# A mixture-of-experts trunk: the index products of a later turn moved from before the down products to behind the transposes

## Chip, cores and metric

One core of a Trainium2 chip runs the whole program in one launch. The metric is the device time in microseconds, the median of several runs. Inputs, weights and arithmetic are f32, except for small one-hot and index tables in bf16.

## What is computed

The reference is a trunk of two layers on 1024 tokens of 1024 features. The first layer mixes tokens with windowed attention, the second with a Fourier transform, and both end with a mixture of 64 experts, of which each token takes 8. The change lies in the experts alone:

```
flat_e = top_e.reshape(-1)
order = jnp.argsort(flat_e)
e_s, tok_s, w_s = flat_e[order], flat_tok[order], flat_w[order]
...
def body(y, b):
    rows = lax.dynamic_slice_in_dim(tok_buf, b * MOE_BLOCK, MOE_BLOCK)
    wb = lax.dynamic_slice_in_dim(w_buf, b * MOE_BLOCK, MOE_BLOCK)
    e = block_e[b]
    xb = x_pad[rows]
    hb = jax.nn.silu(xb @ w_gate[e]) * (xb @ w_up[e])
    return y.at[rows].add((hb @ w_down[e]) * wb[:, None]), None
```

## The kernel before

**Turns.** The routed rows are packed into turns of 128 rows, 71 a layer, in the order of a table (`ORDER`) that gives the experts and of a table (`UNITS`) that gives each expert's rows in units of 32. `schedule` packs them; a turn holds the rows of one or two experts. `pieces` cuts a turn into column tiles of TensorE: one piece 128 wide if the turn has one expert, else pieces 64 or 32 wide. The width is a matter of each turn, so that neighbouring turns and the turn four ahead often have different widths. Rows beyond the tables' capacities go through a loop behind the last turn, which a table of overflow blocks steers.

**One turn b on TensorE** (the block `pe` of `experts`, loop at L1811): `gate_up(b, par, range(SPLIT))`, the first five of eight column steps of gate and up (L1750, 512 columns each, f32, into `exG`); `turn_hidden(b - 1)`, two transposes of the hidden rows of the turn before (L1772, `exH`); the last three column steps of gate and up; `index(b + 4)`, the small products that give the row numbers and weights of the turn four ahead (L1718, `exI`, 6 columns in bf16, 8 steps for each piece); and `down(b - 1)`, the down products (L1784, `exD`). For the turn T - 4 `index_over` takes the place of `index` (L1727).

**What stands around it.** `index(b + 4)` waits for the one-hot tile that DVE makes (`onehot`, L1502, in the trace `mod<-place,slots`; `onehot_over`, L1509, for the last), and for the copy of the index products before (L1517). DVE's turn is `onehot(b + 4)`, `turn_blocks(b + 2)` (L1538), `hidden(b)` (L1543 to L1547, after gate and up of turn b and ACT's exponential, L1683), `indices(b + 4)` (L1517 to L1525), `targets(b - 1)` (L1583) and `weigh(b - 1)` (L1576). In turn 9 `overflow()` stands ahead of `onehot`, 25 small instructions (L1592 to L1617). ACT's turn is `turned(b - 1)`, which copies the transposed hidden rows for down (L1688), `gates(b)` (L1683) and `move(b + 2)` (L1671). POOL gathers the rows of later turns by `indices` and adds the weighed rows into DRAM. SP loads an expert's gate and up weights once the turn that used that ring slot last is through gate and up, and its down weights once that turn's down is through. All of this is written out by hand; the same order of the calls holds on every engine whatever the data.

The loop's order on TensorE is in these lines:

```
gate_up(b, par, range(SPLIT))
turn_hidden(b - 1, 1 - par)
gate_up(b, par, range(SPLIT, KT))
...
if b + AHEAD < T:
    index(b + AHEAD, par)
...
down(b - 1)
```

Of the kernel before, what the change touches and what calls it, by code (L numbers as in the profile page):

```python
# [26 lines left out]
KT = D // P  # L27
# [71 lines left out]
def after(eng, sem, s, lag):  # L99

    if not isinstance(s, int) or s >= lag:
        eng.wait_ge(sem, s - lag + 1)
# [35 lines left out]
def pieces(turn):  # L138

    m = P if len(turn) == 1 else 2 * UNIT if turn[1][3] == 2 * UNIT else UNIT  # L140
    return [(s, r, p, m) for s, r, _, at, n in turn for p in range(at, at + n, m)]
# [61 lines left out]
def trunk(nc, A, out):  # L203
# [9 lines left out]
    with ExitStack() as whole:  # L213
# [1141 lines left out]
        def experts(layer, place, moving, ids, skey, ring, slots, small, w_in, wd_in, load_in, load_down, expert, spent,  # L1355
# [4 lines left out]
            T = len(turns)  # L1360
            GP, GB = T % 2, T // 2
            with ExitStack() as ctx:
# [31 lines left out]
                HAND, AHEAD, SPLIT, Q = 2, 4, 5, P // UNIT  # L1394
# [10 lines left out]
                def columns_ready(eng, b):  # L1405

                    if isinstance(b, int) and HAND <= b < T:
                        eng.wait_ge(moved, b - HAND + 1)
                    else:
                        n = b + 1 if isinstance(b, int) and b < HAND else b - T + 1 + HAND  # L1410
                        eng.wait_ge(xT_a, n)
                        eng.wait_ge(xT_d, n)

                def row(eng, g, c, hi):
                    return eng.value_load(table[0:1, ds(g * 4 + c, 1)], min_val=0, max_val=hi)
# [5 lines left out]
                with nc.Block(no_gpsimd_drain=True) as block:  # L1421
# [75 lines left out]
                    def _(dve):  # L1497
                        def onehot(b, par):

                            after(dve, idx_mm, b, 2)  # L1500
                            for _, r, start, at, n in turns[b]:
                                last = dve.tensor_tensor(hot[:, par, :, at:at + n], place[:, :, r:r + 1].to_broadcast([P, NT, n]),  # L1502
                                                         slots[:, start:start + n].unsqueeze(1).to_broadcast([P, NT, n]), ALU.is_equal)
                            last.then_inc(hot_done, 1)
# [206 lines left out]
                    def _(pe):  # L1711
                        def index(b, par):
                            pe.wait_ge(hot_done, b + 1)
                            if b >= 1:
                                pe.wait_ge(idx_own, 3 if b == 1 else b * 4 - 2)
                            for t in range(NT):
                                for _, r, p, m in pieces(turns[b]):
                                    last = pe.matmul(psI[p:p + m, 0:6], hot[:, par, t, p:p + m], moving[:, t, r, :],  # L1718
                                                     start=t == 0, stop=t == NT - 1)
                            last.then_inc(idx_mm, 1)  # L1720

                        def index_over(b, g):
                            r = row(pe, g, 0, E - 1)
                            pe.wait_ge(hot_done, b + 1)
                            pe.wait_ge(idx_own, b * 4 - 2)
                            for t in range(NT):
                                last = pe.matmul(psI[:, 0:6], hot[:, GP, t], moving[:, t, ds(r, 1), :].rearrange("p a c -> p (a c)"),  # L1727
                                                 start=t == 0, stop=t == NT - 1)
                            last.then_inc(idx_mm, 1)

                        def turn_rows(b, par, landed_at):
                            pe.wait_ge(gathered[par], landed_at)
                            if not isinstance(b, int) or b > T:
                                columns_ready(pe, b - 1)
                            elif b > 0:
                                columns_ready(pe, min(b - 1, HAND - 1))
                            for k in range(KT):
                                last = pe.transpose(psX[:, k], xg[:, par, k * P:(k + 1) * P], ident[:])
                            last.then_inc(X_mm, 1)

                        def gate_up(b, par, some):
                            if some[0] == 0:
                                for s, _, _, _, _ in turns[b]:
                                    if first[s] == b:
                                        pe.wait_ge(w_in[s % RING], 32 * (s // RING + 1))
                                columns_ready(pe, b)
                                after(pe, h_done, b, 2)
                            for k in some:
                                for s, _, p, m in pieces(turns[b]):
                                    last = pe.matmul(psG[par][p:p + m], xT[:, par, k, p:p + m], ring[s % RING][:, 0:2, k * FF:(k + 1) * FF],  # L1750
                                                     start=k == 0, stop=k == KT - 1)
                            if some[-1] == KT - 1:
                                last.then_inc(g_mm, 1)
# [14 lines left out]
                        def turn_hidden(b, par):  # L1768
                            pe.wait_ge(h_done, b + 1)
                            after(pe, hT_done, b, 1)  # L1770
                            for k in range(FK):
                                last = pe.transpose(psH[:, k * P:(k + 1) * P], hid[:, par, k * P:(k + 1) * P], ident[:])  # L1772
                            last.then_inc(H_mm, 1)

                        def down(b):
                            for s, _, _, _, _ in turns[b]:
                                if first[s] == b:
                                    pe.wait_ge(wd_in[s % RING], 16 * (s // RING + 1))
                            pe.wait_ge(hT_done, b + 1)
                            after(pe, y_done, b, 1)  # L1780
                            for c in range(2):
                                for k in range(FK):
                                    for s, _, p, m in pieces(turns[b]):
                                        last = pe.matmul(psD[p:p + m, c], hT[:, k * P + p:k * P + p + m],  # L1784
                                                         ring[s % RING][:, 2, k * D + c * 512:k * D + (c + 1) * 512],
                                                         start=k == 0, stop=k == FK - 1)
                            last.then_inc(d_mm, 1)
# [23 lines left out]
                        for b in range(1, T):  # L1811
                            par = b % 2
                            gate_up(b, par, range(SPLIT))
                            turn_hidden(b - 1, 1 - par)
                            gate_up(b, par, range(SPLIT, KT))
                            if b + 1 == T:
                                turn_rows(T, 1 - par, (T // 2 + 1) * 16)
                            if b + AHEAD < T:
                                index(b + AHEAD, par)
                            elif b + AHEAD == T:  # L1820
                                pe.wait_ge(table_in, 16)
                                index_over(T, 0)
                            down(b - 1)
                        turn_hidden(T - 1, 1 - GP)
                        down(T - 1)
# [545 lines left out]
```

## Time and profile before

| | us |
|---|---|
| median of 3 runs | 2861.16 |
| lowest and highest | 2856.9, 2862.29 |
| profiled execution, its own time | 2862.66 |
| its span | 2860.8 |
| TensorE busy in the span | 2691.1 (94%) |
| DVE busy | 1847.5 (65%) |
| ACT busy | 1350.4 (47%) |
| mean granted clock of TensorE | 0.976 |

The experts take the span from about 770 to 1586 us in the first layer and from about 1980 to 2801 in the second. A matmul's end is modelled in the profile, so that the duration of a row of the timeline is longer than the time to the next product: distances between starts are what counts. A row of the timeline that merges several products gives the first start, the time to the last one's end and their count (an f32 product of 512 columns stands there as two).

### The profile page before, as it was taken

What the parts mean: (1) busy time and instruction counts of PE and PEld (TensorE: products, weight loads), DVE (VectorE), ACT (ScalarE), POOL (GpSimd) and SP (SyncE); (2) the same over time, 40 slices, a digit from 0 to 9 for tenths busy, and PEclk for the clock granted to TensorE, in tenths of its full rate; (3) what the DMA queues carried; (4) which work ended last, traced back from release to release, by engine and by line L of the source; (5) the groups of instructions that cost most, each with busy time, mean ns of one, the idle gap of its engine ahead of it and who ended that gap; (6) DMA issues with size and microseconds to landing.
All of it is one profiled execution on the core that took longest, in us unless ns stands there. A gap on an engine that the chain in (4) does not pass through costs nothing. (4 is left out here: it accounts for less than half of the span.)

```text
span 2860.8 us, 40299 instructions
## 1 busy us (share of the span) xinstructions
PE 2691.1 (94%) x14086; PEld 1224.5 (43%) x14087; DVE 1847.5 (65%) x3359; ACT 1350.4 (47%) x3130; POOL 506.4 (18%) x404
## 2 busy tenths in 40 slices
PE   7998999899899999999999698997999999999994
PEld 2444666445333433434434274443333334333332
DVE  4995555566667666666765545666676766666655
ACT  1113555201166666666665340012656666666653
POOL 0000000111022222222222211100222222222212
PEclk9999999999999999999999899998999999999997
DMA  9777300201499999999999622016999999999996
GB/s 356 269 266 214 125 16 8 80 30 45 170 358 349 334 317 349 357 355 344 378 335 309 225 89 87 30 44 238 330 322 329 306 373 358 349 379 294 330 342 206
DMA packets 147092, 714.98 MB, mean 250 GB/s; under 512 B 16702, under 2 KB 22078, under 8 KB 94665
## 3 DMA queue, kind: packets, MB, share of 16 engines
q1 hardware_dynamic: 104252, 556.14, 49.8%
q0 software_dynamic: 42336, 154.16, 21.1%
q8 instruction: 114, 1.87, 0.3%
q10 hardware_dynamic: 304, 2.11, 0.2%
q14 instruction: 86, 0.70, 0.1%
HBM read 597.50 MB, written 114.84 MB: 249 GB/s over the span
## 5 line engine op out<-in xcount | busy, mean ns | idle before, releaser
L1671 ACT ACTIVATE xT<-xt_blocks 32x256 f32<-32x256 f32 x2208 | 913.8, 414 | 43.1 <-DVE xt_blocks L1538 15.6
L1750 PE MATMUL exG<-ring,xT 128*32 128x512 f32 (+2 forms) x2352 | 701.3, 598 | 4.7 <-DMA ring<-in_exp_w_up_dram 4.2
L1750 PEld LDWEIGHTS exG<-ring,xT 128*32 128x32 f32 (+2 forms) x2352 | 232.1, 140 | 311.3 <-issue 306.2
L1784 PE MATMUL exD<-ring,ex_hT 128*32 128x512 f32 (+2 forms) x1176 | 355.9, 605 | 2.4 <-DVE w_o L1576 1.2
L1543 DVE TENSOR_SCALAR ex_e<-ex_e 128x256 f32<-128x256 f32 x142 | 43.3, 305 | 431.0 <-ACT ex_e L1683 403.5
L1544 DVE RECIPROCAL ex_e<-ex_e 128x256 f32<-128x256 f32 x142 | 249.0, 1753 | 4.9
L1683 ACT ACTIVATE ex_e<-exG 128x256 f32<-128x256 f32 x142 | 54.5, 384 | 315.0 <-PE exG L1750 315.0
L1750 PE MATMUL exG<-oT,xT 128*32 128x512 f32 (+2 forms) x592 | 197.7, 599 | 1.3 <-DVE xT L1532 1.3
L1750 PE MATMUL exG<-w_fnet,xT 128*32 128x512 f32 (+2 forms) x608 | 176.9, 600 | 2.3 <-issue 2.3
L1502 DVE TENSOR_TENSOR mod<-place,slots 128x1024 bf16<-128x1024 f32 (+3 forms) x196 | 174.2, 913 | 5.6 <-PEq L234 4.7
L1478 POOL DMA_INDIRECT y_scratch<-w_fnet,idx_out x72 | 120.7, 1677 | 294.3 <-DMA y_scratch<-w_fnet,idx_out 238.4
L1784 PEld LDWEIGHTS exD<-ring,ex_hT 128*32 128x32 f32 (+2 forms) x1176 | 116.2, 141 | 129.1 <-issue 128.1
L1478 POOL DMA_INDIRECT y_scratch<-w_o,idx_out x72 | 121.0, 1680 | 276.2 <-DMA y_scratch<-w_o,idx_out 195.4
L768 DVE TENSOR_REDUCE mx<-pair 128x2 f32<-128x1280 f32 (+1 forms) x64 | 91.2, 1425 | 110.2 <-PE pair L888 110.2
L1688 ACT ACTIVATE ex_hT<-exH 128x256 f32<-128x256 f32 x144 | 55.3, 384 | 215.1 <-PE exH L1772 215.1
L1750 PE MATMUL exG<-w_o,xT 128*32 128x512 f32 (+2 forms) x464 | 153.8, 599 | 0.0
L287 POOL TENSOR_TENSOR rstd<-var,halves 128x1 f32<-128x1 f32 x42 | 63.0, 1500 | 471.2 <-DVE var L273 471.2
L1467 POOL DMA_INDIRECT oT<-u_scratch,idx x72 | 72.1, 1001 | 356.5 <-DVEq L1527 307.5
L1193 ACT ACTIVATE u2T<-mixT 128x1024 f32<-128x1024 f32 x16 | 16.4, 1023 | 250.5 <-PE mixT L1261 250.5
L1467 POOL DMA_INDIRECT fT<-u_scratch,idx x72 | 72.1, 1001 | 349.4 <-DVEq L1527 294.8
L1750 PE MATMUL exG<-fT,xT 128*32 128x512 f32 (+2 forms) x432 | 125.7, 602 | 0.9 <-DVE xT L1532 0.9
L1253 PE MATMUL mixY<-w_fnet,fT 128*128 128x512 f32 x256 | 117.5, 619 | 6.1 <-PEq L234 4.7
(422 smaller groups left out, 4328.2 us busy)
## 6 DMA issues: line engine op xcount, KB each, us to landing
ring<-in_exp_w_gate_dram SPq DMA_DIRECT2D x64, 1024.0 KB
ring<-in_exp_w_up_dram SPq DMA_DIRECT2D x64, 1024.0 KB
ring<-in_exp_w_down_dram SPq DMA_DIRECT2D x64, 1024.0 KB
ada_w<-in_w_ada_dram SPq DMA_DIRECT2D x48, 512.0 KB, 5.5
oT<-in_exp_w_gate_dram SPq DMA_DIRECT2D x17, 1024.0 KB
oT<-in_exp_w_up_dram SPq DMA_DIRECT2D x17, 1024.0 KB
oT<-in_exp_w_down_dram SPq DMA_DIRECT2D x17, 1024.0 KB
fT<-in_exp_w_gate_dram SPq DMA_DIRECT2D x17, 1024.0 KB
```

Source lines behind the costliest of these rows:

```text
L287: pool.tensor_tensor(r["rstd"][:], r["var"][:], halves[:], ALU.pow).then_inc(r["ready"], 1)
L768: dve.tensor_reduce(mx[:, p % 2], pair[p % 2][:, 0:2 * width(p)[1]].rearrange("p (a s) -> p a s", a=2), AX, ALU.max).then_inc(own, 1)
L1253: last = pe.matmul(psY[:, c], src[:, k, t * P:(t + 1) * P], w[:, k, c * 512:(c + 1) * 512], start=k == 0, stop=k == KT - 1)
L1467: pool.indirect_dma_start(out=xg[:, par], out_offset=None, in_=u_dram, in_offset=bass.IndirectOffsetOnAxis(ap=idx[:, par:par + 1], axis=0) ...
L1478: pool.indirect_dma_start(out=y_dram[layer], out_offset=bass.IndirectOffsetOnAxis(ap=idx_out[:, par:par + 1], axis=0), in_=yo[:, par], in_ ...
L1502: last = dve.tensor_tensor(hot[:, par, :, at:at + n], place[:, :, r:r + 1].to_broadcast([P, NT, n]), slots[:, start:start + n].unsqueeze(1 ...
L1544: link(dve.reciprocal(e[:], e[:]))
L1671: last = act.activation(xT[m * UNIT:(m + 1) * UNIT, par, :, a * UNIT:(a + 1) * UNIT], parts[a * UNIT:(a + 1) * UNIT, m], ACT.Copy)
L1683: act.activation(e[:], psG[par][:, 0], ACT.Exp, scale=-1.0).then_inc(e_done, 1)
L1688: act.activation(hT[:], psH[:, 0:FF], ACT.Copy).then_inc(hT_done, 1)
L1750: last = pe.matmul(psG[par][p:p + m], xT[:, par, k, p:p + m], ring[s % RING][:, 0:2, k * FF:(k + 1) * FF], start=k == 0, stop=k == KT - 1)
L1784: last = pe.matmul(psD[p:p + m, c], hT[:, k * P + p:k * P + p + m], ring[s % RING][:, 2, k * D + c * 512:k * D + (c + 1) * 512], start=k = ...
```

## The change

On TensorE, `index(b + AHEAD, par)` (with its variant for the turn T - 4) now stands right behind `turn_hidden(b - 1)` and in front of the last three column steps of gate and up. Nothing is added or taken away, and the waits in front of each product are the same.

```diff
                             gate_up(b, par, range(SPLIT))
                             turn_hidden(b - 1, 1 - par)
-                            gate_up(b, par, range(SPLIT, KT))
-                            if b + 1 == T:
-                                turn_rows(T, 1 - par, (T // 2 + 1) * 16)
                             if b + AHEAD < T:
                                 index(b + AHEAD, par)
                             elif b + AHEAD == T:
                                 pe.wait_ge(table_in, 16)
                                 index_over(T, 0)
+                            gate_up(b, par, range(SPLIT, KT))
+                            if b + 1 == T:
+                                turn_rows(T, 1 - par, (T // 2 + 1) * 16)
                             down(b - 1)
```

How this moves TensorE's instructions, for three turns near the start of the first layer's experts. `exG_9` are gate and up, `exH` the transposes, `exI` the index products, `exD` down; `w_o`, `oT` and `ring` are ring slots with weights.

```order
 L1750 MATMUL exG_9<-w_o,xT 128x512 x5
 L1772 MATMUL exH<-ident,ex_h 128x128 x2
+L1718 MATMUL exI<-moving,mod 32x6 x32
 L1750 MATMUL exG_9<-w_o,xT 128x512 x3
-L1718 MATMUL exI<-moving,mod 32x6 x32
 L1784 MATMUL exD<-oT,ex_hT 128x512 x4
 L1750 MATMUL exG_9<-ring,xT 32x512 x20
 L1772 MATMUL exH<-ident,ex_h 128x128 x2
+L1718 MATMUL exI<-moving,mod 64x6 x16
 L1750 MATMUL exG_9<-ring,xT 32x512 x12
-L1718 MATMUL exI<-moving,mod 64x6 x16
 L1784 MATMUL exD<-w_o,ex_hT 128x512 x4
```

The index products move ahead of the second part of gate and up, and so the neighbours of each group change: gate and up now stand directly in front of down.

On DVE nothing moves. Turn 9 of the first layer in the changed kernel, from the end of the overflow table to the first instructions of `hidden(9)`:

```order
801 L1616 CAST ex_rowi<-ex_rowf 128x4
802 L1617 TENSOR_SCALAR ex_total<-ex_pend 1x1
803 L1502 TENSOR_TENSOR mod<-place,slots 128x1024
804 L1538 STREAM_TRANSPOSE xt_blocks<-oT 128x1024
805 L1543 TENSOR_SCALAR ex_e<-ex_e 128x256
806 L1544 RECIPROCAL ex_e<-ex_e 128x256
807 L1545 TENSOR_TENSOR ex_e<-exG_9,ex_e 128x256
808 L1547 TENSOR_TENSOR ex_h<-ex_e,exG_9 128x128x2
809 L1517 COPY pick<-exI 128x6
```

And the same turn on TensorE in the changed kernel:

```order
649 L1750 MATMUL exG_9<-oT,xT 128x512 x5
650 L1772 MATMUL exH<-ident,ex_h 128x128 x2
651 L1718 MATMUL exI<-moving,mod 128x6 x8
652 L1750 MATMUL exG_9<-oT,xT 128x512 x3
653 L1784 MATMUL exD<-ring,ex_hT 32x512 x3
```

The index products of turn 13, which need the tile of L1502, stand in front of the last three column steps of turn 9's gate and up, where they stood behind them.

## Rows read from the trace of the kernel before

**Rows 1.** Page, part 1: busy time, share of the span and instructions.

```profile
PE 2691.1 (94%) x14086; PEld 1224.5 (43%) x14087; DVE 1847.5 (65%) x3359; ACT 1350.4 (47%) x3130; POOL 506.4 (18%) x404
```

**Rows 2.** Windows, first layer's experts; columns: stretch, us, busy by engine, PEclk, DMA, GB/s.

```profile
856.00:1586.00 730.00, 724.87 (x4144) 287.57 (x4140) 493.78 (x938) 464.58 (x1132) 171.70 (x128) 1.00 0.97 338
```

**Rows 3.** Waits of PE; columns: us in total, times, longest us.

```profile
PE exI L1718 <- DVE mod L1502: 12.5, 4, 3.4
```

**Rows 4.** Timeline, PE and DVE, a plain turn; columns: start us, us, instruction, count.

```profile
1203.00 3.68 PE L1784 MATMUL exD<-oT,ex_hT 128*128 128x512 f32 x8
...
1208.83 1.29 DVE L1502 TENSOR_TENSOR mod<-place,slots 128x256 bf16<-128x256 f32 x2
...
1210.81 0.38 PE L1772 MATMUL exH<-ident,ex_h 128*128 128x128 f32 x2
...
1211.02 2.74 PE L1750 MATMUL exG<-w_o,xT 128*128 128x512 f32 x6
...
1213.69 0.37 PE L1718 MATMUL exI<-moving,mod 128*32 128x6 bf16 x32
```

**Rows 5.** Timeline, PE, joints of two later turns.

```profile
1221.94 0.44 PE L1772 MATMUL exH<-ident,ex_h 128*128 128x128 f32 x2
1222.31 2.80 PE L1750 MATMUL exG<-ring,xT 128*64 128x512 f32 x12
...
1233.28 2.74 PE L1750 MATMUL exG<-oT,xT 128*128 128x512 f32 x6
1235.86 0.34 PE L1718 MATMUL exI<-moving,mod 128*128 128x6 bf16 x8
1236.13 3.65 PE L1784 MATMUL exD<-ring,ex_hT 128*64 128x512 f32 x16
```

**Rows 6.** Timeline, PE, the same joints as the new order has, first layer.

```profile
782.01 1.04 PE L1738 MATMUL exX<-ident,oT 128*128 128x128 f32 x8
...
782.89 0.34 PE L1718 MATMUL exI<-moving,mod 128*128 128x6 bf16 x8
...
786.10 0.35 PE L1718 MATMUL exI<-moving,mod 128*128 128x6 bf16 x8 [2.87 <-DVE mod L1502]
786.32 6.23 PE L1750 MATMUL exG<-w_o,xT 128*128 128x512 f32 x10
...
1544.16 2.74 PE L1750 MATMUL exG<-w_o,xT 128*128 128x512 f32 x6
...
1546.74 3.60 PE L1784 MATMUL exD<-w_o,ex_hT 128*128 128x512 f32 x8
```

**Rows 7.** Timeline, PE and DVE, turn 9, first and second layer.

```profile
882.72 0.38 PE L1772 MATMUL exH<-ident,ex_h 128*128 128x128 f32 x2
...
887.71 1.23 DVE L1502 TENSOR_TENSOR mod<-place,slots 128x1024 bf16<-128x1024 f32 x1
...
889.00 0.35 PE L1718 MATMUL exI<-moving,mod 128*128 128x6 bf16 x8 [3.32 <-DVE mod L1502]
...
2095.91 0.39 PE L1718 MATMUL exI<-moving,mod 128*32 128x6 bf16 x32 [3.42 <-DVE mod L1502]
2096.22 6.38 PE L1784 MATMUL exD<-ring,ex_hT 128*128 128x512 f32 x8
```

**Rows 8.** Windows behind the wait of the first layer's turn 9.

```profile
889.00:890.00 1.00, 1.00 (x16) 0.55 (x20) 1.00 (x1) 0.00 (x0) 0.00 (x0) 0.96 0.97 307
...
893.00:894.00 1.00, 1.00 (x12) 0.30 (x8) 0.88 (x7) 0.96 (x4) 0.00 (x0) 0.83 0.02 8
```

**Rows 9.** Timeline, DVE and PE, turn 1 of the first layer.

```profile
791.48 1.27 DVE L1502 TENSOR_TENSOR mod<-place,slots 128x768 bf16<-128x768 f32 x2
792.39 0.38 PE L1772 MATMUL exH<-ident,ex_h 128*128 128x128 f32 x2
```

**Rows 10.** Timeline, DVE and PE, turn 67 of the first layer.

```profile
1531.41 1.22 DVE L1509 TENSOR_TENSOR mod<-place,slots 128x1024 bf16 x1 [0.46 <-issue]
...
1532.90 0.38 PE L1772 MATMUL exH<-ident,ex_h 128*128 128x128 f32 x2
```

## The prediction

> **What bounds the kernel now.** I read the page first: TensorE is busy 94% of the span and the next engine 65% [rows 1]. Then the windows by stage: in the steady part of the first layer's experts TensorE is busy 724.87 of 730 us at full clock, and DVE 494 and ACT 465 [rows 2]. So in this stage whatever TensorE executes or waits for is paid in full, and what others do is paid only where TensorE stands for it. Then the list of waits: for the one-hot tile that an index product needs (L1502 on DVE), TensorE waits 12.5 us in 4 places [rows 3]. Everything else of the change must be read from the joints between groups of products, in order of time.
>
> **A plain turn** [rows 4]. The transposes start at 1210.81, the last three column steps of gate and up at 1211.02, the index products of the turn four ahead at 1213.69, and the next turn's transposes at 1221.94: 11.13 us a turn. The one-hot tile for the products at 1213.69 was done at 1208.83 + 1.29 = 1210.12. That is 3.6 us before they need it now. In the changed order they stand at 1211.02, which leaves 0.90 us.
>
> **Part 1, the joints of the common turns.** There are 67 such turns in a layer (turns 1 to 67), 134 in all. Before, each has the joints transposes|gate, gate|index, index|down; after, transposes|index, index|gate, gate|down. A joint has a price where the width of the column tile changes. Products of 512 columns follow each other every 2.58 / 6 = 0.43 us (1233.28 to 1235.86) [rows 5], and with that I read the prices:
> - transposes (128 wide) into 64: 1222.31 - 1221.94 - 0.21 = 0.16 us; into 128: nothing (1211.02 - 1210.81 = 0.21, their own work).
> - gate (128) into index (32): 1213.69 - 1211.02 - 2.56 = 0.11 us; into index (128): 0.02.
> - index (128) into down (64): 0.27 us; index into gate of the same width: 786.32 - 786.10 = 0.22 us [rows 6]. So a switch behind the index adds 0.05 to 0.08, and its work is 0.2 us wherever it stands.
> - gate into down with nothing between, both 128: 1546.74 - 1544.16 - 2.56 = 0.02 us. Transposes into index, both 128: 782.89 - 782.01 - 8 x 0.107 = 0.02 us [rows 6].
>
> Transposes into a 32- or 64-wide index is not in the trace: I bound it by 0 and 0.16, and take 0.16, the row with the same thing in front. From the widths in the tables of units the switches are, before: 54 + 71 + 72 = 197; after: 53 + 71 + 91 = 215. Only one kind grows: gate|down has 91 switches where gate|index had 71, for a turn's rows and those of the turn before differ in width more often. 20 more at 0.11 (out of 128) to 0.16 (out of less), less the 0.02 to 0.07 that a joint without a switch costs, is 2.0 us; the kinds that have one fewer give back 0.3. Sum: **+1.7 us**, between 0 and +3.
>
> The Trainium skill bears on this. Under "TensorEngine Tiling (Array Packing)", section Tiling Modes, it says that a change of tiling mode drains the engine. That speaks against the change, by 18 drains. If each were a full one of 0.16, the sum would have 2.9 in place of 1.7; the trace agrees that there is a price, but makes it smaller behind wide tiles and behind the index.
>
> **Part 2, the new wait in the turn with the overflow table.** In turn 9 DVE computes the overflow table (25 small instructions, L1592 to L1617) ahead of the one-hot tile of turn 13, which is done at 887.71 + 1.23 = 888.94 [rows 7]. Before, TensorE had the 2.56 us of gate and up to do until it stood, and waited 3.32 us. Now it stands at 882.72 + 0.21 = 882.93, with those 2.56 us and down behind it in its queue. Nothing else fills the time, so the 2.56 us now come after the wait. And DVE's chain starts when gate and up of the turn before are done. These end a quarter of a us later against the transposes, since the index (0.22 us and its joint) now stands in front of them. So the loss is 2.56 + 0.25 = 2.8 us a layer, the wait grows from 3.3 to 6.1 us, and the same holds in the second layer, where it was 3.42. TensorE bounds the stage, so nothing gives it back. **+5.6 us**, between +4.5 and +6.
>
> **Part 3, the clock behind that wait.** Before, after 3.32 us of standing, TensorE's granted clock was at its half level (1.2 of 2.4 GHz) from near the end of 889:890, where the mean is 0.96, into 893:894 with 0.83 [rows 8]: some 3.4 us of work at half speed, 1.7 lost. In the second layer down took 6.38 us in place of 3.68, 2.7 lost [rows 4, 7]. Standing 6 us, it will come back to work at half clock in both layers. If the clock returned at the same instants as before, the first layer would lose 4.3 / 2 = 2.15 instead of 1.7 and the second what it lost. **+0.5 us**; the bounds are -4.3 (the slow stretch passes while the engine stands, rival B) and +2 (two longer slow stretches).
>
> **Part 4, the first turn.** In turn 1 the one-hot tile of turn 5 is done at 791.48 + 1.27 = 792.75, and the transposes end at 792.39 + 0.21 = 792.60 [rows 9]. **+0.2 us**, and nothing in the second layer.
>
> **What costs nothing, and its cover.** In the other turns the one-hot tile is done before the new place. The room is 0.9 to 1.3 us in nearly all of them, as in [rows 4], and the smallest is that of turn 67 of the first layer, 1532.90 + 0.21 - (1531.41 + 1.22) = 0.48 us [rows 10]. Of this the later chain takes some 0.25 and the signal 0.06 (888.94 to 889.00), so 0.2 us is left in the worst one. If that cover is gone, each tenth costs 0.1 x 134 = 13 us. The other wait of the index products, for the copy of the previous ones, comes before the one-hot tile on DVE. Behind the index, gate and up finish 0.2 to 0.3 us later, and with them ACT's exponential, the gates chain on DVE and SP's loads behind that count; the transposes want that chain 4 us after its end. Down's hidden rows, which ACT copies after the transposes, keep 2.8 us of room. No DMA is added, and down ends where it did.
>
> **The sum.** 1.7 + 5.6 + 0.5 + 0.2 = +8.0 us on the profiled execution's 2862.66, so 2870.7; that execution is 1.5 above the median of 2861.16, so I forecast **2869.2 us**. A measurement of this kernel tells 0.2%, 5.7 us, from no change. The forecast is 0.28%, just outside.
>
> **Rivals.**
> - B, the longer stand swallows the slow clock: parts 1, 2 and 4 stand, part 3 is -4.3. Gives +3.2, 2864.4 us, no change that can be told. For: the slow stretch began 1 us after work resumed in the first layer. Against: in the second it had begun during the stand and still lasted 5 us into the work.
> - C, faster: the index is cheap behind the transposes. The first down product behind an index is followed 0.08 us late (8 products in 3.68 us [rows 4] against 3.60 without an index in front [rows 6]). If neither this (80 turns with a 128-wide gate, 6.4 us) nor the switch out of the transposes (53 x 0.14 = 7.4 us) occurs at the new place, the sum is 8.0 - 13.8 = -5.8, 2855.4 us. The time falls below that of before once a turn gains 6.3 / 134 = 0.05 us, which outweighs parts 2 to 4. Against: the trace has both prices wherever such a joint stands, and index into gate [rows 6] costs what index into down does.
> - D, the cover of 0.2 to 1 us is not there: the one-hot tile holds TensorE in the common turns too, say by 0.3 us, 40 us in all, 2909 us. Against: every room counted is positive after the 0.3 us.
>
> **Chances.** Forecast 0.65 (its own range 2865 to 2873.5), B 0.18, C 0.07, D 0.10. Part of the forecast's lower end lies within 0.2%. So slower 0.62, the same 0.32, faster 0.06. The range takes in the forecast, most of B, and the beginning of D: 2863 to 2876.
>
> **What would show it.** Right: two waits of the index on DVE's one-hot tile of about 6 us where they were 3.3, each followed by half clock; plain turns of 11.1 us; the switches of gate|down at 0.11 to 0.16 and of transposes|index at 0.16. Wrong: many short waits of TensorE on the one-hot tile (D), transposes|index with a switch but without a gap (C), or full clock right after the long stand (B).

## The result and the profile after

| | before | changed |
|---|---|---|
| median, 8 runs each | 2857.68 us | 2866.18 us |
| lowest and highest | 2856.36, 2862.29 | 2864.25, 2869.85 |
| ratio | | 1.0028, 95% interval 1.0017 to 1.0039 |
| span of the profiled execution | 2860.8 us | 2863.1 us |

The change made the kernel slower by 0.28%, 8 us. The forecast was 8.0 us more (2869.2 us, reckoned from a median of three runs, which eight runs put 3.5 us lower). One of the twelve executions of experiment 4 below took 5627 us, for a reason that no trace shows; its ratio leaves that one out. Page, part 1, of the changed kernel, which answers to [rows 1]:

```profile
PE 2690.2 (94%) x14086; PEld 1221.7 (43%) x14087; DVE 1847.5 (65%) x3359; ACT 1350.3 (47%) x3130; POOL 507.3 (18%) x404
```

The busy times are those of before. A reader who stops here sees nothing. The list of waits shows one thing, against [rows 3]:

```profile
PE exI L1718 <- DVE mod L1502: 18.1, 4, 6.3
```

There are still 4 waits on the one-hot tile, so the common turns have none, but they are 5.6 us longer in total. They grew in the two turns 9. Timeline, PE, first and second layer, against [rows 7]:

```profile
881.95 0.38 PE L1772 MATMUL exH<-ident,ex_h 128*128 128x128 f32 x2
888.43 0.37 PE L1718 MATMUL exI<-moving,mod 128*128 128x6 bf16 x8 [6.10 <-DVE mod L1502]
888.66 4.89 PE L1750 MATMUL exG<-oT,xT 128*128 128x512 f32 x6
893.48 0.63 PE L1784 MATMUL exD<-ring,ex_hT 128*32 128x512 f32 x3
...
2096.02 0.39 PE L1718 MATMUL exI<-moving,mod 128*32 128x6 bf16 x32 [6.26 <-DVE mod L1502]
2096.34 5.21 PE L1750 MATMUL exG<-fT,xT 128*128 128x512 f32 x6
2101.39 3.60 PE L1784 MATMUL exD<-ring,ex_hT 128*128 128x512 f32 x8
```

The waits are 6.10 and 6.26 us where they were 3.32 and 3.42. Behind each stand the three column steps that used to run before the wait. They take 4.82 us (888.66 to 893.48) and 5.05 us (2096.34 to 2101.39), where at full clock they need 2.8 at most, because the clock is at its half level. Windows of the first layer's turn 9:

```profile
882.00:888.00 6.00, 0.33 (x3) 0.09 (x1) 5.12 (x22) 0.38 (x1) 1.59 (x1) 0.83 1.02 416
888.00:889.00 1.00, 0.57 (x9) 0.58 (x10) 1.00 (x2) 0.00 (x0) 0.00 (x0) 0.50 1.06 336
...
892.00:893.00 1.00, 1.00 (x3) 0.34 (x1) 0.00 (x0) 0.00 (x0) 0.00 (x0) 0.58 0.05 8
893.00:894.00 1.00, 1.00 (x10) 0.23 (x12) 0.00 (x0) 0.39 (x2) 0.00 (x0) 1.00 0.00 0
```

**A ledger of turns.** From the start of one turn's transposes to the next one's, turn by turn, changed less before: the 127 common turns (turns 2 to 66 but turn 9, and in the second layer but turn 14) +2.14 us in the first layer and +1.66 in the second; turns 9 +3.27 and +2.52; turn 67 +0.69 and +0.09; turn 1 of the first layer -0.52; turn 14 of the second layer -2.26. Sum +7.6 us. That the two spans differ by 2.3 only comes from the stretch between the two layers' experts, from the last transposes of the one to the first of the other. No instruction was moved there. It took 414.9 us before and 409.7 in the changed kernel, and in the other kernels of this study, with the same instructions in it, between 409.7 and 415.7. Most of the difference is TensorE's clock. In the router and shared products of that stretch (L1268 to L1281, from 1761.9 us before and 1765.8 in the changed kernel) the clock fell twice before and not at all after. Windows, first the kernel before, then the changed one at the same places of the program:

```profile
1764.00:1767.00 3.00, 3.00 (x4) 1.22 (x4) 2.34 (x4) 0.22 (x1) 1.52 (x1) 0.50 0.03 5
1801.50:1804.50 3.00, 3.00 (x5) 1.26 (x4) 2.45 (x4) 0.00 (x0) 1.52 (x1) 0.50 0.00 0
...
1768.00:1771.00 3.00, 3.00 (x8) 1.33 (x7) 2.44 (x4) 0.08 (x1) 1.52 (x1) 1.00 0.02 5
1803.70:1806.70 3.00, 3.00 (x9) 1.32 (x8) 2.45 (x4) 0.00 (x0) 1.52 (x1) 1.00 0.00 0
```

From the first of these products to the next group it is 55.4 us before and 52.0 after: 3.4 of the 5.2 us.

Turn 14 of the second layer waits for weights at its end in both kernels, 4.18 and 3.45 us. Before, the clock fell behind the wait and ten products took 6.25 us; in the changed kernel it did not fall:

```profile
2164.41 4.56 PE L1750 MATMUL exG<-ring,xT 128*128 128x512 f32 x10 [3.45 <-DMA ring<-in_exp_w_up_dram]
```

The length of the wait does not decide this: in experiment 4 below the same wait of 3.45 us was followed by the half clock.

```profile
2147.47 6.25 PE L1751 MATMUL exG<-ring,xT 128*128 128x512 f32 x10 [3.45 <-DMA ring<-in_exp_w_up_dram]
```

Between the kernels of this study the turn takes from 14.9 to 19.8 us. That is not all scatter. In the four kernels that have the new order in all turns before it, or in all but turn 9 (the changed one and experiments 1, 4 and 9), the wait ends 10.5 to 10.6 us after the turn's transposes, in the eight others 11.0 to 13.0 us after them. So a part of the -2.26 may belong to the change; no run separates it.

### The profile page after: what moved, and what is told of

It is laid out like the page before. It is cut to its first block and busy times, and to the rows that moved or that the text cites. A ratio compares the mean times of both kernels' runs of the same rounds, so it can differ in the third digit from the quotient of the medians.

```text
span 2863.1 us, 40299 instructions
## 1 busy us (share of the span) xinstructions
PE 2690.2 (94%) x14086; PEld 1221.7 (43%) x14087; DVE 1847.5 (65%) x3359; ACT 1350.3 (47%) x3130; POOL 507.3 (18%) x404
## 5 line engine op out<-in xcount | busy, mean ns | idle before, releaser
L1784 PE MATMUL exD<-ring,ex_hT 128*32 128x512 f32 (+2 forms) x1176 | 349.5, 596 | 2.4 <-DVE w_o L1576 1.3
L1502 DVE TENSOR_TENSOR mod<-place,slots 128x1024 bf16<-128x1024 f32 (+3 forms) x196 | 174.1, 912 | 5.6 <-PEq L234 4.7
```

## Experiments

Experiments 1 and 2 put the turns 9 back or change them alone; 3 and 4 remove the wait; 5 to 8 test the joints; 9 and 10 make the one-hot tile later. Theory 1 is the forecast's: most of the loss is turn 9, the rest the joints. Theory 2 puts it into the joints or a new wait of the common turns.

**1. The old place in turn 9 alone** (and in T - 4).

```diff
+early = b != 9
+if early and b + AHEAD < T:
+    index(b + AHEAD, par)
 gate_up(b, par, range(SPLIT, KT))
...
+if not early and b + AHEAD < T:
+    index(b + AHEAD, par)
```

> The changed order everywhere but in turn 9 (and the last turn with an index, T - 4), where the index products stand in front of down as before. Theory 1 (most of the loss is the overflow turn, whose 2.56 us of gate and up no longer stand ahead of the wait): the two turns 9 go from 19.5 and 20.0 us back to about 16.3 and 17.4, the waits from 6.1 and 6.3 back to about 3.3 to 3.6, and what is left against the kernel before is the joints of the other turns, +3 to +4 us: 2861 to 2862 where before has 2857.7. Theory 2 (the loss is the joints or a wait in common turns, and the turn 9 only moved it): the time stays within 1.5 us of the changed kernel, 2866.

Measured: 1.0009 of before (1.0001 to 1.0018), median 2862.8. Turn 9 of the first layer stands as before, down ahead of nothing but the index:

```profile
886.35 2.74 PE L1750 MATMUL exG<-oT,xT 128*128 128x512 f32 x6
892.53 0.35 PE L1718 MATMUL exI<-moving,mod 128*128 128x6 bf16 x8 [3.45 <-DVE mod L1502]
892.82 0.71 PE L1784 MATMUL exD<-ring,ex_hT 128*32 128x512 f32 x3
```

Two thirds of the loss, 0.19 of 0.28%, go with this one turn, though each ratio is known to 0.1% only. The ledger is sharper: the turns 9 are 3.14 and 3.25 us shorter than in the changed kernel. The second is 0.73 us shorter even than before, with a wait of 3.70 us, since the half clock behind it lasted 3.4 us and not 6.8. The common turns keep +2.15 and +1.39 us.

**2. The new place in turn 9 alone**, with `early = b == 9`.

> The kernel before, with the changed order in turn 9 of each layer alone. Theory 1: turns 9 get 2.5 to 3.3 us longer each, +5 to +6 us in all, 2863 to 2864 where before has 2857.7; common turns as before. Theory 2: under +2 us, within what a measurement can tell. If the clock behind the longer wait comes back at the same time as before, the loss in each is 2.5 to 3 us; if it needs longer, up to 4.

Measured: 1.0020 (1.0009 to 1.0031). The common turns are those of before (+0.01 and +0.03 us in all), the turns 9 +3.41 and +1.78. In the second layer:

```profile
2092.29 0.38 PE L1772 MATMUL exH<-ident,ex_h 128*128 128x128 f32 x2
2098.44 0.39 PE L1718 MATMUL exI<-moving,mod 128*32 128x6 bf16 x32 [5.76 <-DVE mod L1502]
2098.76 4.96 PE L1750 MATMUL exG<-fT,xT 128*128 128x512 f32 x6
2103.55 3.60 PE L1784 MATMUL exD<-ring,ex_hT 128*128 128x512 f32 x8
```

The wait is 0.5 us shorter than in the changed kernel (5.76 for 6.26) and 0.16 in the first layer (5.94 for 6.10). That has the sign that the forecast says, since turn 8 has its index in the old place here and DVE's chain starts earlier against the transposes; the forecast's 0.25 us lies between the two. The two halves add up: 1.0009 and 1.0020 against 1.0028. Theory 2 falls as the explanation of the larger part.

**3 and 4. Take the cause of the wait away.** The overflow table's instructions are given out by a generator, five in each of turns 9 to 13, behind `turn_blocks`, in the old order (3) and in the new (4).

```diff
+table_steps = overflow()
...
-if b == 9:
-    overflow()
...
 if b + 2 < T:
     turn_blocks(b + 2, par)
+if 9 <= b < 15:
+    for _ in range(5):
+        next(table_steps, None)
 hidden(b, par, 2)
```

> The kernel before, with the overflow table's 25 instructions on DVE cut into five pieces of five, one in each of turns 9 to 13 behind the transposes of the rows, where DVE waits about 3 us in every turn. Both theories: no wait on the one-hot tile in turn 9 and no fall of the clock behind it, so that turns 9 are 11.1 us instead of 16.3 and 17.4: -11.5 us, 2846. A rival: the pieces push DVE's chain back in each of the five turns and cost some tenths in each, -9 us.

> The changed kernel with the overflow table in the same five pieces. Theory 1: turns 9 fall from 19.5 and 20.0 us to 11.1, -17 us, 2849; against the old order with the same pieces only the joints are left, +3 to +4 us (0.13%). Theory 2: more than +6 us against the old order with the same pieces. A rival: pieces of 1 to 2 us in DVE's turn take away the 0.5 to 1 us of room of the one-hot tile in turns 10 to 14, with new waits there; then under -15 us.

Measured: old order 0.9961 (0.9948 to 0.9973), new order 0.9981 (0.9973 to 0.9990). Timeline, DVE, turn 9 of the first layer in the old order:

```profile
883.00 0.69 DVE L1597 TENSOR_REDUCE ex_nblk<-logits 128x64 f32<-128x512 f32 x1
884.47 0.29 DVE L1543 TENSOR_SCALAR ex_e<-ex_e 128x256 f32<-128x256 f32 x1 [0.78 <-ACT ex_e L1684]
```

After the five largest instructions DVE still waits 0.78 us for ACT, so they cost nothing. Turns 9 are 5.18 and 6.19 us shorter than before, the 11.5 us expected, while turn 14 of the second layer is 2.6 us longer, with a longer wait for weights (6.19 us). And the list of waits has only the start of the layers left, the same in both orders:

```profile
PE exI L1719 <- DVE mod L1502: 5.7, 2, 2.9
```

In the new order they are 8.35 and 8.72 us shorter than in the changed kernel, the 17 us expected; the whole time fell by less than that, from 1.0028 to 0.9981 of the kernel before, some 13 us. Of the difference 1.7 us are turn 14 of the second layer; the rest I can't place. No turn 9 differs between the two orders now by more than 0.1 us. Against each other they show what is left of the change: common turns +2.15 and +1.55 us, turn 67 +0.86 and +0.44, turn 1 +0.72. The rival of the taken-away room did not come: no wait in turns 10 to 14.

**What the joints cost.** With waits and clock out of the way, each common turn can be compared by the widths of its gate and up (turn b), of its index (turn b + 4) and of its down products (turn b - 1). New less old order, experiments 4 and 3, the 127 common turns, median of each kind:

| gate | index | down | turns | us |
|---|---|---|---|---|
| any | any | 128 | 77 | -0.02 to +0.03 |
| 128 | 128 | 32 or 64 | 25 | +0.10 |
| 128 | 32 | 32 | 11 | +0.25 |
| 128 | 32 | 64 | 3 | +0.19 |
| 32 | 128 | 32 | 2 | -0.24 |
| 32 | 64 | 32 | 2 | -0.14 |
| 32 | 32, or 128 with down 64 | 32 or 64 | 6 | -0.09 to -0.12 |
| 64 | 64 | 32 | 1 | +0.02 |

**5. Choose the place turn by turn.** From both traces I made prices for each joint and took the new place in the 21 turns of a layer where they made it cheaper.

> The old order with the spread overflow table, but in 21 turns of each layer the changed place of the index: those where the joints' prices, as both traces show them (a switch 0.11 to 0.16 us, and 0.10 more for the second product when a group 128 wide follows the index or a switch), make it the cheaper one. If the prices are right, -4.3 us against the old order with the spread table (0.15%), some 2842. If the extra tenth is no matter of the switch into a 128-wide group, the gain is under 1.5 us.

Measured: 0.9953 (0.9940 to 0.9967); the common turns gave -0.77 and -0.79 us, a third of what I expected. The price list was wrong for narrow gates in front of 128-wide down products: 34 of the 42 picked turns are of that kind, and by the table above they gain nothing. The other eight gave 1.2 us. The whole time can't be told from that of experiment 3.

**6 to 8. The table as a rule.** New place only in turns with a 128-wide gate and narrower down (6), in all others but T - 4 (7), and the old order again (8), in one call.

```diff
+early = pieces(turns[b])[0][3] == P and pieces(turns[b - 1])[0][3] < P
```

> The old order with the spread table, with the changed place of the index only in the 41 turns whose gate and up are 128 wide while the down products behind them are 64 or 32 wide. Theory 3 (a group 128 wide behind the index or a switch pays a tenth more, and in these turns the changed order makes one more such group): each of the 41 turns gets 0.10 us longer with a 128-wide index and 0.17 to 0.26 with a 32-wide one, as in the two traces with the spread table; 5.6 us in all, against the old order with the spread table. Theory 1 as it was put before (the price is the number of switches, gate and down together): all turns share it, 41 of 134 get some 1.2 us.

> The old order with the spread table, with the changed place of the index in all turns but those 41 (and T - 4). Theory 3: the 80 turns with 128-wide down products stay as they are, the 11 with narrow gate and narrow down get 0.1 to 0.25 us shorter: -1.5 us against the old order with the spread table, 0.05%, and the best of all versions. Theory 1 as it was put before: +2.5 us.

> The old order with the spread table once more, as the ground for the other two: 0.996 of the kernel before, common turns equal to those of its first run within 0.02 us each.

Measured against before: 0.9980 (0.9971 to 0.9989), 0.9960 (0.9947 to 0.9974), 0.9955 (0.9942 to 0.9969). By turns, against experiment 3: (6) +3.06 and +2.56, 5.62 us where 5.6 was expected; (7) -0.89 and -0.90, 1.8 us for 1.5 expected; (8) -0.02 and +0.31, which is how far such a sum can be trusted. The time of (6) is clear of (8); (7) can't be told from it by its time. One turn shows the mechanism. Timeline, PE, turn 38 of the first layer, in experiment 3:

```profile
1203.86 0.38 PE L1773 MATMUL exH<-ident,ex_h 128*128 128x128 f32 x2
1204.08 2.74 PE L1751 MATMUL exG<-w_o,xT 128*128 128x512 f32 x6
1206.75 0.37 PE L1719 MATMUL exI<-moving,mod 128*32 128x6 bf16 x32
1206.97 0.59 PE L1785 MATMUL exD<-oT,ex_hT 128*32 128x512 f32 x1
...
1210.56 4.51 PE L1751 MATMUL exG<-ring,xT 128*64 128x512 f32 x20
```

and in experiment 6:

```profile
1208.37 0.38 PE L1773 MATMUL exH<-ident,ex_h 128*128 128x128 f32 x2
1208.68 0.36 PE L1719 MATMUL exI<-moving,mod 128*32 128x6 bf16 x32
1208.98 2.84 PE L1751 MATMUL exG<-w_o,xT 128*128 128x512 f32 x6
1211.75 0.62 PE L1785 MATMUL exD<-oT,ex_hT 128*32 128x512 f32 x1
...
1215.32 4.51 PE L1751 MATMUL exG<-ring,xT 128*64 128x512 f32 x20
```

From the transposes to the next gate: 6.70 us in the old order, 6.95 in the new. Old: gate straight behind the transposes, 0.22; one switch out of gate, 0.11; index and down are both 32 wide. New: a switch into the index (0.31 where the gate followed after 0.22), a switch out of it (0.30 where down followed after 0.22), and the gate's six products take 2.84 and not 2.74, that is, the second one comes 0.10 late; then again the 0.11 out of gate. 0.09 + 0.08 + 0.10, less 0.02 in the down row, are the 0.25. In the 25 turns with a 128-wide index, and in turn 9 of the first layer, there is no switch more than in the old order. Their +0.10 is 0.08 for the late second product, and 0.02 because the switch into down costs 0.09 behind gate and cost 0.07 behind the index.

**9 and 10. How near is the cliff.** `onehot` and `turn_blocks` change places on DVE, in the new order (9) and in the old (10).

```diff
+if b + 2 < T:
+    turn_blocks(b + 2, par)
 if b + AHEAD < T:
     onehot(b + AHEAD, par)
...
-if b + 2 < T:
-    turn_blocks(b + 2, par)
```

> The changed kernel, with DVE's one-hot tile made behind the transposes of the rows (1.25 us later in each turn). The room of the one-hot tile was 0.5 to 1.0 us in the changed order, so theory: TensorE waits 0.3 to 0.7 us on it in nearly every turn, common turns get about 11.6 instead of 11.1 us, 134 x 0.45 = +60 us on the changed kernel, 2925. Rival: the one-hot tile is no condition that matters in common turns; no change.

> The kernel before, with the same swap on DVE. The room there is 3.6 us, so 1.25 us later costs nothing in common turns; in turns 9 the index waits 1.25 us longer each, +2.5 us, 2860. Rival: the earlier transposes of the rows let ACT's copies start earlier, up to -1 us.

Measured: 1.0957 (1.0940 to 1.0973) for the new order, 1.0019 (1.0010 to 1.0028) for the old. In the new order TensorE now waits in every turn, and much longer than I expected:

```profile
PE exI L1718 <- DVE mod L1502: 226.2, 133, 7.4
```

Timeline of one such turn, ACT, DVE and PE:

```profile
1311.61 6.80 ACT L1671 ACTIVATE xT<-xt_blocks 32x256 f32<-32x256 f32 x16
...
1318.51 1.25 DVE L1538 STREAM_TRANSPOSE xt_blocks<-oT 128x1024 f32<-128x1024 f32 x1 [1.32 <-ACT xT L1671]
1318.91 0.38 PE L1772 MATMUL exH<-ident,ex_h 128*128 128x128 f32 x2
...
1319.67 1.18 DVE L1502 TENSOR_TENSOR mod<-place,slots 128x1024 bf16<-128x1024 f32 x1
...
1320.91 0.36 PE L1718 MATMUL exI<-moving,mod 128*128 128x6 bf16 x8 [1.62 <-DVE mod L1502]
```

I had counted the 1.25 us of `turn_blocks` and not what it waits for: ACT's 6.80 us of copies, which start when gate and up are done. The one-hot tile now hangs on them (1318.51 waits 1.32 us for ACT), and since gate and up hang on the index in the new order, the circle closes: copies, transposes, one-hot tile, index, second part of gate and up, exponential, copies. It is 12.8 us long (1311.61 to 1324.40, where the next copies start), and TensorE has only 11.1 us of work for it. In the old order gate and up of the same turn do not wait for the index that stands behind them, and the common turns did not change (+0.06 and -0.21 us). What it cost there is turn 9 (+0.95 and +0.58), turn 67 of the first layer (+0.52) and, not expected, turn 1 of the first layer (+4.46), where the one-hot tile now stands behind a `turn_blocks` that waits for gathered rows:

```profile
799.64 1.25 DVE L1538 STREAM_TRANSPOSE xt_blocks<-oT 128x1024 f32<-128x1024 f32 x1 [3.84 <-DMA oT<-u_scratch,idx]
```

## Why the forecast was right, point by point

- **What bounds the kernel**: right, with one doubt. The losses in the common turns and in the turns 9 stand in the span turn by turn; only turn 14 of the second layer, where TensorE waits for weights, is 2.26 us shorter, and how much of that the change gave back is not shown.
- **Part 2, the wait in turn 9** (+5.6 forecast): right in size and in mechanism. The waits grew by 2.78 and 2.84 us where the text had 2.56 + 0.25. Experiments 1 and 2 give the two turns 0.19 and 0.20% of the time, 5.4 and 5.7 us. That the later chain adds to the wait is seen in experiment 2, where 0.16 and 0.50 us are missing.
- **Part 3, the clock** (+0.5): TensorE came back at half clock as forecast, but that cost nothing more than before. By the rows, the first layer lost 2.05 us to the half clock for 1.7 before, the second some 2.3 for 2.7: 0 in sum. Rival B, that the long stand swallows the slow stretch, is out: in both kernels with the long wait TensorE came back at half clock, in both layers.
- **Part 1, the joints** (+1.7): the mis-sized term; it measured +3.8 us in the changed kernel and +3.7 with the spread table. The step that failed is "Only one kind grows": I charged the switches and nothing else, and saw the late second product only as rival C's 0.08 us, which I took to fall as often in either order. It falls on a 128-wide group behind the index (0.08 us) or behind a switch (0.10). Where down is 128 wide, both orders pay it once, and they have equally many switches: these turns did not change. A turn with a wide gate and narrow down pays it in the new order alone: 41 turns, 3.3 to 4.1 us by these two prices. Transposes into a 32-wide index cost 0.10, less than the 0.16 that I took. The Trainium skill's rule ("TensorEngine Tiling (Array Packing)", Tiling Modes) is that a change of tiling mode drains the engine. It agrees with the sign of every kind of turn whose number of switches changed: -0.24 us for two fewer, +0.25 for two more. But by that count the 26 turns with a wide gate, a wide index and narrow down are free, and they cost 2.6 us, more than the 2.1 that the forecast lacked.
- **Part 4, turn 1** (+0.2): right in mechanism, about 0.1 in size. In the changed kernel the index starts 0.40 us after the transposes, 0.05 after the one-hot tile is done, where a 128-wide group into a 32-wide index without a wait has 0.31. In experiment 1, with the same order, the tile came 0.7 us later against the transposes and the wait cost 0.8. The turn as a whole (-0.5 us here, +1.2 in experiment 1) also holds the wait of its next gate and up, which was 0.54 us before, nothing in the changed kernel and 0.9 in experiment 1.
- **What costs nothing**: the common turns have no new wait. But turn 67, which I counted among those with room (0.48 us), cost 0.69 us in the first layer and 0.09 in the second: a term that the forecast put at nothing. Its index products take their addresses from a register. In the first layer they took 0.79 us from their start to the next group:

```profile
1537.25 0.38 PE L1772 MATMUL exH<-ident,ex_h 128*128 128x128 f32 x2
1537.47 0.93 PE L1727 MATMUL exI<-moving,mod 128*128 x8
1538.26 2.82 PE L1750 MATMUL exG<-w_o,xT 128*128 128x512 f32 x6
```

  The one-hot tile was done at 1537.19, some 0.3 us ahead. No run was made for this, but the other traces show the pattern. The eight products start 0.025 us apart when the tile was done long before, and a slow one starts 0.124 us behind the one ahead of it:

| kernel, layer | tile done ahead of the first product, us | slow starts | first product to next group, us |
|---|---|---|---|
| experiment 4, first | 0.14 | all 7 | 0.94 |
| changed, first | 0.29 | all but the first, one partly | 0.79 |
| experiment 4, second | 0.44 | the last 5, one partly | 0.74 |
| experiment 10, first | 0.48 | the last 4, one partly | 0.79 |
| changed, second | 0.79 | the last | 0.38 |
| experiment 10, second | 1.18 | none | 0.22 |
| before, first and second | 3.07, 3.77 | none | 0.27, 0.22 |

  The later the tile, the more products are slow, also in the old place (experiment 10). Index products with fixed addresses show nothing of it: in experiment 9 they waited for the tile to the last and took 0.22 us (1320.91 to 1321.13). So it goes with the register addresses; what in the engine takes the 0.124 us is not shown.
- **Rival C** fell: the index is not cheap behind the transposes. **Rival D** did not happen: no common turn waits, and in turn 67 of the first layer, the smallest room, 0.3 us were left. Experiment 9 does not price it in the order as forecast, but shows that a one-hot tile 1.25 us later costs 2 us in every turn, through a path over ACT that D did not have.

The sum came out at 8.0 for 8.0 partly by luck: the joints were 2 us too low, the clock half a us too high, turn 67 was missing, and turn 14 and the stretch between the layers moved by 2.3 and 5.3 us, which the forecast did not have at all.

## What to carry to other kernels

An item that waits for another engine's late product belongs behind work that needs no wait, not in front of it: the same wait then covers 2.6 us less, and in the circle through the other engines each turn has less room. Before adding a wait, write down what the releasing instruction itself waits for, since a circle that closes over a third engine sets the length of every turn as soon as it is longer than the work in the turn (12.8 against 11.1 us in experiment 9). And a rare turn with extra work on a side engine is worth a look: cutting 25 small instructions into five idle gaps gave 0.4%, more than any place of the index.

## What the runs showed of the hardware

- The second of a row of f32 products with 128 x 128 weights starts 0.08 us late when the row follows the 6-column index products, and 0.10 us late when it follows a switch of the column tile (six products in 2.84 us for 2.74). It is not late when the row follows the 128-wide transposes or another 128-wide row. Behind a switch the second column step of 64-wide pieces starts 0.05 us late, that of 32-wide pieces 0.02.
- Eight index products with addresses from a register start 0.025 us apart when what they wait for was done 1.2 us or more ahead, and up to all of them 0.124 us apart when it was done 0.14 us ahead.
- Between two executions with the same instructions, sums over the common turns differ by 0.02 to 0.3 us, while the whole time scatters by 5 us and more (2854.6 to 2866.5 us in 25 executions of the kernel before). Turn sums from one profile told differences of 1.5 us that five rounds of timing could not.
- The length of a wait does not by itself decide whether the clock falls: after 3.45 us of waiting for weights in turn 14 of the second layer it stayed at full level in the changed kernel and fell in experiment 4. After the waits of 3.3 to 7.4 us in the turns 9 it was at its half level, or fell to it within 1.4 us, in every kernel that had such a wait.
